# A DiT layer on one core: the second norm and the first seven-part product in another order on VectorE and ScalarE, two low parts on GpSimd

## The chip, the core and the metric

The kernel runs on one core of one Trainium2 chip. The metric is the time of one execution on the device, in microseconds (us). For the kernel before, it is 1764.85 us, the median of 3 runs that lie between 1764.47 and 1765.17 us.

## The reference

One layer of a diffusion backbone on 1024 latent tokens of width 1024, with 256 context tokens. Its first half (a recurrent branch, a windowed attention branch, their merge and the output projection) ends in the stream `x`. The change lies behind it, in the second half:

```python
x = x + g1 * merge_branches(y_rx, y_ax, gax, gbx, w_o_rnn[l], w_o_attn[l], w_out[l])
hx2 = modulate(rms_norm(x, norm2_w[l]), sh2, sc2)
x = x + g2 * conv_ffn(hx2, w_up[l], ffn_conv_w[l], ffn_conv_b[l], w_down[l])
...
def conv_ffn(h, w_up, conv_w, conv_b, w_down):
    u = dwconv(h @ w_up, conv_w, conv_b, FFN_CONV_W // 2)
    a, v = jnp.split(u, 2, axis=-1)
    return (jax.nn.gelu(a) * v) @ w_down
```

`h @ w_up` has 2 x 3072 output columns. The kernel holds channels on the partitions: a "row" is 128 channels x 1024 tokens, and rows come in 24 pairs of a gate row and a value row.

## The kernel before

**The split.** Every fp32 matrix product is made as three fp32r matmuls (lines 921 to 923): high x high, high x low, low x high. So every operand needs a high part (a rounding copy, mostly on ScalarE) and a low part (source minus high part, mostly on VectorE), and a tile can enter TensorE only when both are there.

**The second norm.** VectorE adds the projection to the stream (`add_out_half`, L2577), in halves of 512 tokens for the last two rows. The sums of squares go through TensorE (`square_columns`, L1333); VectorE adds them (`second_sum`, L2600), ScalarE takes the root (`second_root`), VectorE builds a diagonal from the reciprocal (`second_diagonal`, L2608), and TensorE spreads it over the partitions into PSUM (`spread`, L1343, two matmuls L1347 and L1348). This is done once for each half h of the tokens. Then for each of 8 row blocks k VectorE scales the stream (`normed`, L2590, tile yq), ScalarE makes the high part with the shift added (`normed_high`, tile B_hi), and VectorE the low part (`normed_low`, L2597, tile B_lo). For h = 0, `second_sum(1)` and `second_diagonal(1)` for the other half stand between these, ahead of k = 5 and k = 6.

**The plain products.** The first two pairs of rows are made as plain products (`plain_part`, L1364). Pair 0 follows the norm block by block, for h = 0 and then h = 1; `spread(1)` stands ahead of its k = 7. Pair 1 follows in one piece of 96 matmuls and needs its weights' high parts from ScalarE (`high_w`) and their low parts from VectorE (`plain_low`, L2653, tile wlo_both).

**The seven-part products.** The other 22 pairs are made by a seven-product scheme on 2 x 2 blocks (`fast_pair`, L1393). Each of the seven parts is 12 matmuls: 4 blocks x three matmuls. One operand is a block of the normed stream or one of the sums T1 to T4 (built once, tile T_sum, `t1f` to `t3f` and the lower left of yq), the other a weight block or a sum of two (`weight_sums`, tile wsum, lines 2700 to 2705), with high and low part (`fac_high`, `fac_low` L2711). The parts are taken in the order B11, T2, T3, T1, B21, T4, B22. The first product also needs T2, T3, T1 and T4 in high (`block_high`) and low parts (`block_low`, L2672), all four low parts on VectorE; T1, T2 and T3 have theirs written over the sums. ScalarE makes the high parts of the fifth and sixth weight block only behind the low part of T4.

**Around each pair**, ScalarE writes the centre tap of the convolution (tiles ca and cv), VectorE adds the two other taps (`taps_of` L2686 and L2689, `value_taps_of` L2715 and L2718), ScalarE applies GELU, VectorE multiplies (`product_of`, L2724), and the SP queue stores the row (`store_row`, L640). `up_step` (L2789 on VectorE, L2039 on ScalarE) writes out this order for the pairs from the second on. The centre of the next value row waits for the product before it, and the centre of the next gate row for the store to land.

Engines run their lists in written order and meet only at semaphores. `t_sum` counts the sums, `t_hi` and `t_lo` the high and low parts of the T blocks. In `fast_pair` the first product's waits are:

```python
if f in (1, 2, 3, 5):
    pe.wait_ge(S["t_lo"], AT["t_lo"] + {1: 1, 3: 2, 2: 3, 5: 4}[f])
```

GpSimd's last work in the kernel before is `add_half_square(1)` (L891), at about 1011 us.

Of the kernel before, what the change touches and what calls it, by code (L numbers as in the profile page):

```python
# [73 lines left out]
def build(nc, D, out):  # L74
# [199 lines left out]
    with ctx:  # L274
# [446 lines left out]
        def _(pool):  # L721
# [190 lines left out]
            add_half_square(1)  # L912


        @block.tensor
        def _(pe):
# [457 lines left out]
            for h in range(2):  # L1374
                for k in range(KC):
                    if h == 0 and k == 3:
                        square_columns(1)
                    elif h == 0 and k == KC - 1:
                        spread(1)
# [100 lines left out]
        def _(act):  # L1480
# [461 lines left out]
            normed_high(0, range(3, 5))  # L1942
            second_root(1)
            normed_high(0, range(5, KC))
# [3 lines left out]
            normed_high(1, range(KC))  # L1948
# [7 lines left out]
            block_high(T3, t3f[:, :, :], 4 * KQ)  # L1956
# [29 lines left out]
            gelu_of(0)  # L1986
            for f in (1, 2, 3):
                fac_high(1, 0, f)
            act.wait_ge(S["plain_full"], AT["plain_full"] + 3)
            act_of(ug[:, :], plain_row(1, 0), ACT.Copy).then_inc(S["row_copied"], 1)  # L1990
            act.wait_ge(S["plain_full"], AT["plain_full"] + 4)
            act_of(uv[:, :], plain_row(1, 1), ACT.Copy).then_inc(S["row_copied"], 1)
            block_high(T4, yq[:, KQ:, 0:HALF], 4 * KQ)
            for f in (4, 5):
                fac_high(1, 0, f)
# [120 lines left out]
        def _(dve):  # L2116
# [513 lines left out]
            for k in range(1, KC):  # L2630
                if k == 3:
                    add_out_half(KC - 1, 1)
                elif k == 5:
                    second_sum(1)
                elif k == 6:
                    second_diagonal(1)
# [13 lines left out]
            link(v.tensor_tensor(sh_diff[:, :], rest[:, 1, KQ:], rest[:, 1, 0:KQ], sub))  # L2650
            for k in range(KQ):
                v.tensor_tensor(t1f[:, k, :], yq[:, k, HALF:SEQ], yq[:, k, 0:HALF], sub).then_inc(S["t_sum"], 1)
# [5 lines left out]
            for c in range(2):  # L2658
                plain_low(c)
# [4 lines left out]
            for k in range(KQ):  # L2664
                dve.wait_ge(S["t_sum"], AT["t_sum"] + KQ + k + 1)
                v.scalar_tensor_tensor(out=yq[:, k + KQ, 0:HALF], in0=yq[:, k + KQ, 0:HALF],
                                       scalar=rest[:, 1, k + KQ:k + KQ + 1], in1=t2f[:, k, :], op0=add, op1=sub)\
                    .then_inc(S["t_sum"], 1)
# [4 lines left out]

            for k in range(KQ):
                v.scalar_tensor_tensor(out=t3f[:, k, :], in0=yq[:, k + KQ, HALF:SEQ], scalar=sh_diff[:, k:k + 1],
                                       in1=yq[:, k, HALF:SEQ], op0=add, op1=sub).then_inc(S["t_sum"], 1)
            dve.wait_ge(S["t_sum"], AT["t_sum"] + 3 * KQ)
            block_low(T2, t2f[:, :, :], 1)
            block_low(T1, t1f[:, :, :], 2)
# [273 lines left out]
```

## Time and profile before

| | us |
|---|---|
| median of 3 runs | 1764.85 |
| the profiled execution, on the device | 1765.58 |
| its span in the trace | 1763.8 |
| TensorE (matmul) busy | 1730.7 |
| VectorE busy | 1220.7 |
| ScalarE busy | 776.0 |
| GpSimd busy | 542.6 |

Times in the trace count from the start of the span. PE is TensorE, DVE is VectorE, ACT is ScalarE, POOL is GpSimd, SP is the queue that issues most transfers. The granted TensorE clock is full in all 40 slices of the span. Matmuls of 512 columns overlap, so a row's duration (0.39 us) is longer than the distance of two starts; places are therefore compared here by their start times. Where a row has a count above 1, its duration is that of the whole group.

### The profile page before, as it was taken

What the parts mean: (1) busy time and instruction counts of PE and PEld (TensorE: products, weight loads), DVE (VectorE), ACT (ScalarE), POOL (GpSimd) and SP (SyncE); (2) the same over time, 40 slices, a digit from 0 to 9 for tenths busy, and PEclk for the clock granted to TensorE, in tenths of its full rate; (3) what the DMA queues carried; (4) which work ended last, traced back from release to release, by engine and by line L of the source; (5) the groups of instructions that cost most, each with busy time, mean ns of one, the idle gap of its engine ahead of it and who ended that gap; (6) DMA issues with size and microseconds to landing.
All of it is one profiled execution on the core that took longest, in us unless ns stands there. A gap on an engine that the chain in (4) does not pass through costs nothing.

```text
span 1763.8 us, 23344 instructions
## 1 busy us (share of the span) xinstructions
PE 1730.7 (98%) x8382; PEld 1433.7 (81%) x8382; DVE 1220.7 (69%) x1386; ACT 776.0 (44%) x1017; POOL 542.6 (31%) x262
## 2 busy tenths in 40 slices
PE   7999999999999999989999999999999999999998
PEld 5897888887888888878888877888888888888887
DVE  7989767779316588867246389999999898424425
ACT  6358778788000288830011144444444444202205
POOL 1037766664336576625557700000000000000000
PEclk9999999999999999999999999999999999999999
DMA  9231111111453300057216312222222224523112
GB/s 370 78 114 45 51 52 51 61 52 43 167 193 96 84 13 0 1 197 248 80 59 251 124 54 96 84 95 83 88 78 83 78 82 161 203 105 128 54 37 96
DMA packets 56149, 177.98 MB, mean 101 GB/s; under 512 B 11794, under 2 KB 12178, under 8 KB 55444
## 3 DMA queue, kind: packets, MB, share of 16 engines
q1 hardware_dynamic: 46964, 148.27, 23.8%
q10 hardware_dynamic: 9120, 28.84, 5.0%
q8 instruction: 41, 0.67, 0.2%
q14 instruction: 24, 0.20, 0.0%
HBM read 140.39 MB, written 31.46 MB: 97 GB/s over the span
## 4 chain that ended last, share of the span: by engine, by line
PE 80%; DVE 7%; issue 2%; ACT 2%; DMA 1%; POOL 0%; SPq 0%; ACTq 0%; DVEq 0%; POOLq 0%
PE acc L921 17%; PE acc L922 17%; PE acc L923 17%; PE gp L921 8%; PE gp L922 8%; PE gp L923 8%; PE gp L1071 2%; PE acc L1249 1%; DMA wst<-in_w_in 1%; DVE r_lo L2353 1%; DVE y_lo L2371 1%; DVE T_lo L2672 0%; PE gp L1224 0%; PE gp L1223 0%; PE gp L1222 0%
## 5 line engine op out<-in xcount | busy, mean ns | idle before, releaser
L921 PE MATMUL acc<-hx_hi,whi_both 128*128 128x512 f32 x672 | 264.4, 393 | 3.5 <-ACT sg L1482 1.6
L922 PE MATMUL acc<-hx_lo,whi_both 128*128 128x512 f32 x672 | 261.8, 390 | 0.0
L923 PE MATMUL acc<-hx_hi,wlo_both 128*128 128x512 f32 x672 | 261.5, 389 | 0.0
L731 POOL TENSOR_TENSOR whi_both<-wst,ones 128x1024 fp32r<-128x1024 f32 x56 | 148.3, 2648 | 258.6 <-PE acc L923 244.8
L733 POOL TENSOR_TENSOR wlo_both<-wst,whi_both 128x1024 fp32r<-128x1024 f32 x56 | 174.2, 3111 | 4.4
L921 PEld LDWEIGHTS acc<-hx_hi,whi_both 128*128 128x128 f32 x672 | 126.1, 188 | 35.7 <-issue 4.6
L923 PEld LDWEIGHTS acc<-hx_hi,wlo_both 128*128 128x128 f32 x672 | 126.2, 188 | 26.6
L922 PEld LDWEIGHTS acc<-hx_lo,whi_both 128*128 128x128 f32 x672 | 126.2, 188 | 25.0
L1482 ACT ACTIVATE dn_hi<-wst 128x768 fp32r<-128x768 f32 x32 | 26.9, 844 | 182.8 <-PE acc L923 120.9
L921 PE MATMUL acc<-T_hi,fac_hi 128*128 128x512 f32 x264 | 102.8, 389 | 0.4 <-DVE fac_lo L2711 0.4
L923 PE MATMUL acc<-T_hi,fac_lo 128*128 128x512 f32 x264 | 102.7, 389 | 0.0
L922 PE MATMUL acc<-T_lo,fac_hi 128*128 128x512 f32 x264 | 102.7, 389 | 0.0
L2786 DVE SCALAR_TENSOR_TENSOR x1t<-acc,rest,x1t 128x1024 f32<-128x1024 f32 x16 | 20.5, 1281 | 101.8 <-PE acc L923 101.8
L921 PE MATMUL gp<-g_hi,dn_hi 128*128 128x512 f32 x192 | 74.9, 390 | 1.0 <-DVE dn_lo L2779 1.0
L922 PE MATMUL gp<-g_lo,dn_hi 128*128 128x512 f32 x192 | 74.7, 389 | 0.0
L923 PE MATMUL gp<-g_hi,dn_lo 128*128 128x512 f32 x192 | 74.7, 389 | 0.0
L921 PE MATMUL acc<-g_hi,dn_hi 128*128 128x512 f32 x192 | 74.7, 389 | 0.0
L922 PE MATMUL acc<-g_lo,dn_hi 128*128 128x512 f32 x192 | 74.7, 389 | 0.0
L923 PE MATMUL acc<-g_hi,dn_lo 128*128 128x512 f32 x192 | 74.7, 389 | 0.0
L1482 ACT ACTIVATE fac_hi<-wsum 128x512 fp32r<-128x512 f32 x88 | 51.8, 625 | 49.7 <-DVE wsum L2703 40.9
L921 PE MATMUL gp<-B_hi,fac_hi 128*128 128x512 f32 x176 | 68.5, 389 | 0.0
L922 PE MATMUL gp<-B_lo,fac_hi 128*128 128x512 f32 x176 | 68.5, 389 | 0.0
(403 smaller groups left out, 4624.6 us busy)
## 6 DMA issues: line engine op xcount, KB each, us to landing
wst<-in_w_in SPq DMA_DIRECT2D x43, 512.0 KB, 3.5
wst<-in_w_up SPq DMA_DIRECT2D x26, 512.0 KB, 4.2
wg<-in_mod_rest ACTq DMA_DIRECT2D x24, 512.0 KB, 5.3
ffn_row_scratch<-ca SPq DMA_DIRECT2D x24, 512.0 KB, 2.6
wst<-in_w_down SPq DMA_DIRECT2D x32, 384.0 KB, 3.1
g_in<-ffn_row_scratch SPq DMA_DIRECT2D x24, 512.0 KB, 7.0
wup<-in_w_up SPq DMA_DIRECT2D x22, 512.0 KB, 4.0
wmod<-in_mod_first SPq DMA_DIRECT2D x16, 512.0 KB, 15.5
```

Of the source, the lines that this page charges most:

```text
L731: nc.gpsimd.tensor_tensor(whi[s][:, 0:kc, :], wst[s][:, 0:kc, :], ones_of(kc), mult).then_inc(S["w_hi"], 1)
L733: nc.gpsimd.tensor_tensor(wlo[s][:, 0:kc, :], wst[s][:, 0:kc, :], whi[s][:, 0:kc, :], sub)\
L921: mm(out_ap, w_h, x_h, start=first, stop=False)
L922: mm(out_ap, w_h, x_l, start=False, stop=False)
L923: return mm(out_ap, w_l, x_h, start=False, stop=last)
L1071: last = mm(bank[:, o:o + wide], w[rows, d, :], x[rows, x0:x0 + wide], start=t == 0, stop=t == 2)
L1249: last = nc.tensor.transpose(pt_bank(j)[:, P * h:P * (h + 1)], prob[kh][:, h, P * kb:P * (kb + 1)], ident[:, :])
L1482: return nc.scalar.activation(o, x, f, **kw)
L2353: v.tensor_tensor(r_lo[c][:, :], Y[:, c, :], r_hi[c][:, :], sub).then_inc(S["y_lo_s"], 1)
L2371: v.tensor_tensor(dst[:, c, :], src[:, c, :], hi[:, c, :], sub).then_inc(S[lo_sem], 1)
L2786: v.scalar_tensor_tensor(out=x1t[m][:, :], in0=o_bank(n), scalar=rest[:, 3, m:m + 1], in1=x1t[m][:, :], op0=mult, op1=add).then_inc(S["dn_ ...
```

## The change

It changes no arithmetic result of any tile, only the order of instructions and, for two of them, the engine.

- Second norm, first half: `second_sum(1)` and `second_diagonal(1)` stand one block later on VectorE (ahead of k = 6 and k = 7); `spread(1)` one block earlier on TensorE (ahead of k = 6); on ScalarE the root stands behind one more high part.
- ScalarE makes the high parts of the second half's blocks 0 to 2 ahead of the first weight copy, and block 3 between the two copies.
- VectorE makes the first plain low part ahead of the sums T1, and the sums T3 ahead of the sums T4.
- The low parts of T1 and T3 are made by GpSimd, behind the low part of T2, which stays on VectorE.
- VectorE makes the weight sums and the first weight blocks' low parts, with T2's, ahead of the taps of pair 0; the product of pair 0 stands behind the low parts of T4 and of weight blocks 4 and 5.
- ScalarE copies the first row of pair 1 ahead of weight blocks 1 to 3, and the GELU of pair 0 stands behind T4's high part.

```diff
--- before.py
+++ after.py
@@ -910,6 +910,10 @@
             for c in range(2):
                 split_plain(c)
             add_half_square(1)
+            pool.wait_ge(S["t_lo"], AT["t_lo"] + 1)
+            for blk, total, count in ((T1, t1f, 2), (T3, t3f, 3)):
+                pool.wait_ge(S["t_hi"], AT["t_hi"] + count)
+                nc.gpsimd.tensor_tensor(blk[1][:, :, :], total[:, :, :], blk[0][:, :, :], sub).then_inc(S["t_lo"], 1)
 
 
         @block.tensor
@@ -1375,7 +1379,7 @@
                 for k in range(KC):
                     if h == 0 and k == 3:
                         square_columns(1)
-                    elif h == 0 and k == KC - 1:
+                    elif h == 0 and k == KC - 2:
                         spread(1)
                     for c in range(2):
                         last = plain_part(0, c, h, (k,), plain_hi[c], plain_lo[c])
@@ -1939,13 +1943,15 @@
             half_square(KC - 2, 1)
             normed_high(0, range(3))
             half_square(KC - 1, 1)
-            normed_high(0, range(3, 5))
+            normed_high(0, range(3, 6))
             second_root(1)
-            normed_high(0, range(5, KC))
+            normed_high(0, range(6, KC))
+            normed_high(1, range(3))
             full(act, A_S5 + KC - 1)
             for c in range(2):
                 high_w(W_S6 + 2 + c, "w_ready", W_S6 + 2)
-            normed_high(1, range(KC))
+                normed_high(1, (3 + c,))
+            normed_high(1, range(5, KC))
 
             def block_high(blk, src, sums):
                 act.wait_ge(S["t_sum"], AT["t_sum"] + sums)
@@ -1953,7 +1959,7 @@
 
             block_high(T2, t2f[:, :, :], 2 * KQ)
             block_high(T1, t1f[:, :, :], KQ)
-            block_high(T3, t3f[:, :, :], 4 * KQ)
+            block_high(T3, t3f[:, :, :], 3 * KQ)
 
             def centre_of(p, src):
                 act_of(ca[:, :], src, ACT.Identity, scale=conv_col(1, 0, p), bias=ffn_col(C_FCB, p)).then_inc(S["f_centre"], 1)
@@ -1983,14 +1989,14 @@
             act.wait_ge(S["plain_full"], AT["plain_full"] + 2)
             value_centre_of(0, plain_row(0, 1))
             fac_high(1, 0, 0)
-            gelu_of(0)
+            act.wait_ge(S["plain_full"], AT["plain_full"] + 3)
+            act_of(ug[:, :], plain_row(1, 0), ACT.Copy).then_inc(S["row_copied"], 1)
             for f in (1, 2, 3):
                 fac_high(1, 0, f)
-            act.wait_ge(S["plain_full"], AT["plain_full"] + 3)
-            act_of(ug[:, :], plain_row(1, 0), ACT.Copy).then_inc(S["row_copied"], 1)
             act.wait_ge(S["plain_full"], AT["plain_full"] + 4)
             act_of(uv[:, :], plain_row(1, 1), ACT.Copy).then_inc(S["row_copied"], 1)
             block_high(T4, yq[:, KQ:, 0:HALF], 4 * KQ)
+            gelu_of(0)
             for f in (4, 5):
                 fac_high(1, 0, f)
             act.wait_ge(S["row_copied"], AT["row_copied"] + 2)
@@ -2630,9 +2636,9 @@
             for k in range(1, KC):
                 if k == 3:
                     add_out_half(KC - 1, 1)
-                elif k == 5:
+                elif k == 6:
                     second_sum(1)
-                elif k == 6:
+                elif k == 7:
                     second_diagonal(1)
                 normed(0, k)
                 normed_low(0, k - 1)
@@ -2647,38 +2653,27 @@
 
             dve.wait_ge(S["n2_a"], 2 * KC)
             dve.sem_inc(acc_read[A_ST2 % 2], 1)
-            link(v.tensor_tensor(sh_diff[:, :], rest[:, 1, KQ:], rest[:, 1, 0:KQ], sub))
-            for k in range(KQ):
-                v.tensor_tensor(t1f[:, k, :], yq[:, k, HALF:SEQ], yq[:, k, 0:HALF], sub).then_inc(S["t_sum"], 1)
             def plain_low(c):
                 n0 = W_S6 + 2 + c
                 dve.wait_ge(S["w_hi"], n0 + 1)
                 v.tensor_tensor(wlo[n0 % 2][:, :, :], wst[n0 % 2][:, :, :], whi[n0 % 2][:, :, :], sub).then_inc(S["w_ready"], 1)
 
-            for c in range(2):
-                plain_low(c)
+            plain_low(0)
+            link(v.tensor_tensor(sh_diff[:, :], rest[:, 1, KQ:], rest[:, 1, 0:KQ], sub))
+            for k in range(KQ):
+                v.tensor_tensor(t1f[:, k, :], yq[:, k, HALF:SEQ], yq[:, k, 0:HALF], sub).then_inc(S["t_sum"], 1)
+            plain_low(1)
             for k in range(KQ):
                 dve.wait_ge(S["t_sum"], AT["t_sum"] + k + 1)
                 v.scalar_tensor_tensor(out=t2f[:, k, :], in0=yq[:, k + KQ, HALF:SEQ], scalar=rest[:, 1, k + KQ:k + KQ + 1],
                                        in1=t1f[:, k, :], op0=add, op1=sub).then_inc(S["t_sum"], 1)
             for k in range(KQ):
-                dve.wait_ge(S["t_sum"], AT["t_sum"] + KQ + k + 1)
-                v.scalar_tensor_tensor(out=yq[:, k + KQ, 0:HALF], in0=yq[:, k + KQ, 0:HALF],
-                                       scalar=rest[:, 1, k + KQ:k + KQ + 1], in1=t2f[:, k, :], op0=add, op1=sub)\
-                    .then_inc(S["t_sum"], 1)
+                v.scalar_tensor_tensor(out=t3f[:, k, :], in0=yq[:, k + KQ, HALF:SEQ], scalar=sh_diff[:, k:k + 1],
+                                       in1=yq[:, k, HALF:SEQ], op0=add, op1=sub).then_inc(S["t_sum"], 1)
 
             def block_low(blk, src, count):
                 dve.wait_ge(S["t_hi"], AT["t_hi"] + count)
                 v.tensor_tensor(blk[1][:, :, :], src, blk[0][:, :, :], sub).then_inc(S["t_lo"], 1)
-
-            for k in range(KQ):
-                v.scalar_tensor_tensor(out=t3f[:, k, :], in0=yq[:, k + KQ, HALF:SEQ], scalar=sh_diff[:, k:k + 1],
-                                       in1=yq[:, k, HALF:SEQ], op0=add, op1=sub).then_inc(S["t_sum"], 1)
-            dve.wait_ge(S["t_sum"], AT["t_sum"] + 3 * KQ)
-            block_low(T2, t2f[:, :, :], 1)
-            block_low(T1, t1f[:, :, :], 2)
-            dve.wait_ge(S["t_sum"], AT["t_sum"] + 4 * KQ)
-            block_low(T3, t3f[:, :, :], 3)
 
             def taps_of(p, src):
 
@@ -2723,15 +2718,25 @@
                 dve.wait_ge(S["v_conv"], AT["v_conv"] + p + 1)
                 v.tensor_tensor(ca[:, :], ca[:, :], cv[:, :], mult).then_inc(S["f_prod"], 1)
 
+            for k in range(KQ):
+                dve.wait_ge(S["t_sum"], AT["t_sum"] + KQ + k + 1)
+                v.scalar_tensor_tensor(out=yq[:, k + KQ, 0:HALF], in0=yq[:, k + KQ, 0:HALF],
+                                       scalar=rest[:, 1, k + KQ:k + KQ + 1], in1=t2f[:, k, :], op0=add, op1=sub)\
+                    .then_inc(S["t_sum"], 1)
+            weight_sums(1, 0)
+            fac_low(1, 0, 0)
+            dve.wait_ge(S["t_sum"], AT["t_sum"] + 4 * KQ)
+            block_low(T2, t2f[:, :, :], 1)
+            fac_low(1, 0, 1)
+            for f in (2, 3):
+                fac_low(1, 0, f)
             taps_of(0, plain_row(0, 0))
-            weight_sums(1, 0)
-            for f in range(4):
-                fac_low(1, 0, f)
             value_taps_of(0, plain_row(0, 1))
-            product_of(0)
+            dve.wait_ge(S["t_lo"], AT["t_lo"] + 3)
             block_low(T4, yq[:, KQ:, 0:HALF], 4)
             for f in (4, 5):
                 fac_low(1, 0, f)
+            product_of(0)
 
             def top_right(e, i):
```

VectorE, second norm of the first half, before: `COPY` and the next row are `second_sum(1)`, the rows from `RECIPROCAL` to `diag_lo` are `second_diagonal(1)`; yq rows are `normed`, B_lo rows `normed_low`.

```order
516 L2603 COPY rstd_61<-gp 128x4
517 L2606 TENSOR_TENSOR rms<-gp,rstd_61 128x4
518 L2590 SCALAR_TENSOR_TENSOR yq<-yq,a2col,acc 128x512
519 L2597 SCALAR_TENSOR_TENSOR B_lo<-yq,rest,B_hi 128x512
520 L2612 RECIPROCAL rstd_61<-rms 128x4
```

The same place in the changed kernel:

```order
516 L2596 SCALAR_TENSOR_TENSOR yq<-yq,a2col,acc 128x512
517 L2603 SCALAR_TENSOR_TENSOR B_lo<-yq,rest,B_hi 128x512
518 L2609 COPY rstd_61<-gp 128x4
519 L2612 TENSOR_TENSOR rms<-gp,rstd_61 128x4
520 L2596 SCALAR_TENSOR_TENSOR yq<-yq,a2col,acc 128x512
521 L2603 SCALAR_TENSOR_TENSOR B_lo<-yq,rest,B_hi 128x512
522 L2618 RECIPROCAL rstd_61<-rms 128x4
```

One `normed` and one `normed_low` now stand ahead of the sum that they followed.

VectorE, from the end of the norm to the first weight block's low part, before (T_sum and yq x4 are the sums T1, T2, T4, T3):

```order
543 L2650 TENSOR_TENSOR sh_diff<-rest 128x4
544 L2652 TENSOR_TENSOR T_sum<-yq 128x512 x4
545 L2656 TENSOR_TENSOR wlo_both<-wst_74,whi_both 128x1024
546 L2656 TENSOR_TENSOR wlo_both<-wst_73,whi_both 128x1024
547 L2662 SCALAR_TENSOR_TENSOR T_sum<-yq,rest,T_sum 128x512 x4
548 L2666 SCALAR_TENSOR_TENSOR yq<-yq,rest,T_sum 128x512 x4
549 L2675 SCALAR_TENSOR_TENSOR T_sum<-yq,sh_diff 128x512 x4
550 L2672 TENSOR_TENSOR T_lo<-T_sum,T_hi 128x2048 x3
551 L2686 SCALAR_TENSOR_TENSOR ca<-gp,pcol,ca 128x1023
552 L2689 SCALAR_TENSOR_TENSOR ca<-gp,pcol,ca 128x1023
553 L2700 TENSOR_TENSOR wsum_255<-wst_74 128x512
```

The changed kernel:

```order
554 L2706 TENSOR_TENSOR fac_lo_248<-wst_73,fac_hi_241 128x512
555 L2676 TENSOR_TENSOR T_lo<-T_sum,T_hi 128x2048
556 L2706 TENSOR_TENSOR fac_lo_249<-wsum_256,fac_hi_242 128x512
557 L2706 TENSOR_TENSOR fac_lo_250<-wsum_257,fac_hi_243 128x512
558 L2706 TENSOR_TENSOR fac_lo_251<-wsum_255,fac_hi_244 128x512
559 L2681 SCALAR_TENSOR_TENSOR ca<-gp,pcol,ca 128x1023
560 L2684 SCALAR_TENSOR_TENSOR ca<-gp,pcol,ca 128x1023
561 L2710 SCALAR_TENSOR_TENSOR cv<-gp,pcol,cv 128x1023
562 L2713 SCALAR_TENSOR_TENSOR cv<-gp,pcol,cv 128x1023
563 L2676 TENSOR_TENSOR T_lo<-yq,T_hi 128x2048
564 L2706 TENSOR_TENSOR fac_lo_252<-wst_73,fac_hi_245 128x512
565 L2706 TENSOR_TENSOR fac_lo_253<-wst_74,fac_hi_246 128x512
```

Ahead of these stand, in the changed kernel, one plain low part, `sh_diff`, the four sums T1, the other plain low part, the sums T2, T3 and T4 and the four weight sums. Of the three low parts of T1 to T3 one is left on VectorE. The other two are the last rows of GpSimd:

```order
227 L896 TENSOR_TENSOR ssum<-ssum,sqb 128x512
228 L916 TENSOR_TENSOR T_lo<-T_sum,T_hi 128x2048 x2
229 L274 UNCONDITIONAL_BRANCH
```

Nothing moved ahead of them: GpSimd has been out of work since the half square.

## Rows read from the trace of the kernel before

**Rows 1.** The page: busy time of each engine, then the chain that ended last, by engine.

```profile
PE 1730.7 (98%) x8382; PEld 1433.7 (81%) x8382; DVE 1220.7 (69%) x1386; ACT 776.0 (44%) x1017; POOL 542.6 (31%) x262
...
PE 80%; DVE 7%; issue 2%; ACT 2%; DMA 1%; POOL 0%; SPq 0%; ACTq 0%; DVEq 0%; POOLq 0%
```

**Rows 2.** Who waited for whom: TensorE from 975 to 1100 us (total, times, longest).

```profile
PE gp L921 <- DVE B_lo L2597: 2.5, 2, 1.5
PE acc L921 <- DVE wlo_both L2656: 1.4, 1, 1.4
```

**Rows 3.** The timeline: TensorE (start, duration; in brackets idle before it and its releaser).

```profile
1024.94 0.50 PE L921 MATMUL gp<-B_hi,plain_hi 128*128 128x512 f32 x1 [1.48 <-DVE B_lo L2597]
...
1030.83 0.50 PE L921 MATMUL gp<-B_hi,plain_hi 128*128 128x512 f32 x1 [1.02 <-DVE B_lo L2597]
...
1043.47 0.47 PE L921 MATMUL acc<-B_hi,whi_both 128*128 128x512 f32 x1 [1.45 <-DVE wlo_both L2656]
...
1065.11 0.39 PE L923 MATMUL acc<-B_hi,wlo_both 128*128 128x512 f32 x1
1066.09 0.47 PE L921 MATMUL acc<-B_hi,fac_hi 128*128 128x512 f32 x1 [0.60 <-ACT ug L1482]
...
1088.54 0.50 PE L921 MATMUL acc<-T_hi,fac_hi 128*128 128x512 f32 x1 [0.41 <-DVE fac_lo L2711]
```

**Rows 4.** The timeline: VectorE, from the second norm to the second product.

```profile
1019.38 0.16 DVE L2603 COPY rstd<-gp 128x4 f32<-128x4 f32 x1 [1.48 <-PE gp L1331]
...
1025.46 1.63 DVE L2597 SCALAR_TENSOR_TENSOR B_lo<-yq,rest,B_hi 128x512 fp32r<-128x512 f32 x2
1028.49 1.41 DVE L2590 SCALAR_TENSOR_TENSOR yq<-yq,a2col,acc 128x512 f32<-128x512 f32 x2 [1.39 <-PE acc L1348]
...
1039.69 2.50 DVE L2652 TENSOR_TENSOR T_sum<-yq 128x512 f32<-128x512 f32 x4
1042.11 2.35 DVE L2656 TENSOR_TENSOR wlo_both<-wst,whi_both 128x1024 fp32r<-128x1024 f32 x2
...
1052.33 6.68 DVE L2672 TENSOR_TENSOR T_lo<-T_sum,T_hi 128x2048 fp32r<-128x2048 f32 x3
...
1061.44 0.68 DVE L2700 TENSOR_TENSOR wsum<-wst 128x512 f32<-128x512 f32 x1
...
1063.97 0.69 DVE L2711 TENSOR_TENSOR fac_lo<-wst,fac_hi 128x512 fp32r<-128x512 f32 x1
1064.58 1.89 DVE L2711 TENSOR_TENSOR fac_lo<-wsum,fac_hi 128x512 fp32r<-128x512 f32 x3
...
1069.08 1.22 DVE L2724 TENSOR_TENSOR ca<-ca,cv 128x1024 f32<-128x1024 f32 x1
1070.22 2.28 DVE L2672 TENSOR_TENSOR T_lo<-yq,T_hi 128x2048 fp32r<-128x2048 f32 x1
...
1075.44 0.69 DVE L2711 TENSOR_TENSOR fac_lo<-wsum,fac_hi 128x512 fp32r<-128x512 f32 x1 [0.89 <-ACT fac_hi L1482]
...
1087.81 1.89 DVE L2711 TENSOR_TENSOR fac_lo<-wsum,fac_hi 128x512 fp32r<-128x512 f32 x3
```

**Rows 5.** Groups by line and shape: GpSimd (count, busy us, mean ns).

```profile
L825 POOL TENSOR_TENSOR q_lo<-yq,q_hi 128x512 fp32r<-128x512 f32 x16 | 20.8, 1298 | 2.3 <-POOL q_hi L823 1.8
...
L904 POOL TENSOR_TENSOR plain_lo<-wst,plain_hi 128x1024 fp32r<-128x1024 f32 x2 | 4.8, 2392 | 0.2
```

**Rows 6.** The timeline: VectorE from 957.5 to 962 us.

```profile
957.56 3.22 DVE L2513 SCALAR_TENSOR_TENSOR wgr<-wgr,crow 128x1024 f32<-128x1024 f32 x1
...
960.71 1.27 DVE L2574 SCALAR_TENSOR_TENSOR yq<-acc,rest,xres 128x1024 f32<-128x1024 f32 x1
```

**Rows 7.** The timeline: GpSimd in the same stretch.

```profile
959.78 3.27 POOL L733 TENSOR_TENSOR wlo_both<-wst,whi_both 128x1024 fp32r<-128x1024 f32 x1
```

**Rows 8.** The timeline: ScalarE, centre of the second value row.

```profile
1073.66 1.23 ACT L1482 ACTIVATE cv<-uv,pcol 128x1024 f32<-128x1024 f32 x1
```

**Rows 9.** DMA issues from 1498.9 to 1499.2 us (count, KB each, us to landing).

```profile
ffn_row_scratch<-ca SPq DMA_DIRECT2D x1, 512.0 KB, 3.1
```

## The prediction

> **What bounds the kernel now.** I read the page first. TensorE is busy 98% of the span and holds 80% of the chain that ended last [rows 1]. The change gives TensorE no matmul more or less, so it can win only time in which TensorE stands still between its units of work. The second view is who waited for whom on TensorE around the change: 2.5 us for low parts of the norm and 1.4 us for a plain low part [rows 2]. The third, TensorE's own timeline, says where: it restarts late at 1024.94, 1030.83 and 1043.47, at 1066.09 (the first seven-part product) and at 1088.54 (second part of the second one). The idle times there are 1.48, 1.02, 1.45, 0.60 and 0.41 us, together 5.0 us, 0.28% of the span [rows 3]. Four of the five name VectorE. So the last view is VectorE's timeline. The reader is to see that it runs from 1028.49 to 1088.5 with two pauses only, one of them 0.89 us at 1075.44 [rows 4]. The last stop, at 1088.54, is where that list and TensorE meet for the last time: whatever TensorE gains before, it gives back there unless VectorE arrives earlier too. I therefore compute that meeting twice, and the change of the time is its shift; behind it both kernels run the same lists, and the waits of TensorE up to the down projection end with it.
>
> **Norm, second half.** VectorE stands idle for 1.48 us ahead of the row at 1019.38, since it needs the columns from TensorE, which are not moved. One `normed` and one `normed_low` now fall into that pause: 2 x 0.66 us of starts (half of a pair that takes 1.41 and 1.63 us with overlap). Its first half then ends at 1025.46 + 1.63 - 1.3 = 1025.8. The spread stood ahead of k = 7 and is now ahead of k = 6; its diagonal is ready where it was, three starts of 0.66 us ahead of the row at 1025.46, at about 1023.6; TensorE is then in k = 5, so the spread is done by 1024.8, and VectorE goes on at 1025.8 with no wait, where it began at 1028.49 [rows 4]: 2.7 us earlier. TensorE followed that start by 1030.83 - 1028.49 = 2.34 us, so it starts the half at 1028.1. Of the wait at 1024.94 I expect some 0.3 us left, in front of k = 6.
>
> **Plain rows of pair 1.** The two weight copies on ScalarE now stand between high parts; that pushes VectorE by at most a copy's overlap, which I take as 0.2 us. TensorE needs 48 x 0.227 = 10.9 us for the half; the 0.227 comes from 1043.47 to 1065.11, 95 starts of a 96-matmul product, less the slow first [rows 3]. It is through at 1039.0. The plain low part comes first on VectorE now, at 1025.8 + (1039.69 - 0.19 - 1028.49) + 0.2 = 1037.0, and is there at 1038.2: the wait of 1.45 us is gone. The 96 matmuls start at 1039.0 where they started at 1043.47, and end at 1060.8. The wait of 0.60 us for the copied row goes as well, since ScalarE copies it at 1053 and TensorE comes at 1060.8, 5.3 us earlier than 1066.09.
>
> **VectorE up to T2's low part.** From 1028.49 to the three low parts at 1052.33 it needed 23.84 us; the same list now runs from 1025.8 to 1049.8. Weight sums 1063.97 - 1061.44 = 2.5 us, half a us for ScalarE, whose high parts come first, the first weight block 0.6, T2's low part 2.2 (a third of 6.68 us) [rows 4]: 1055.6.
>
> **The low parts on GpSimd.** No row shows a 128x2048 subtraction there. 128x512 takes 1298 ns and 128x1024 2392 ns [rows 5], so 1.09 us for each 512 more, 4.6 us for 2048 and 9.2 us for two, against 2.2 us each that VectorE saves. The rows also show that the two engines slow each other: a VectorE operation with two inputs in SBUF took 3.22 us beside GpSimd [rows 6], where two plain low parts of the same size took 2.35 us together [rows 4], and GpSimd took 3.27 instead of 2.39 us [rows 7]. An operation with one input in PSUM took 1.27 us beside the same GpSimd row [rows 6]: not slowed. GpSimd starts at 1055.7. Three weight low parts of 512 fall beside it: VectorE needs 1.6 instead of 0.6 us for each, 4.9 us together, and GpSimd loses 3 x 0.44 = 1.3 us. The four taps of pair 0 read PSUM, so they cost their old 2.5 + 2.6 us. VectorE is ready for T4 at 1065.7; GpSimd ends at 1055.7 + 9.2 + 1.3 = 1066.2, and VectorE waits half a us for it. The bounds of the term: 9.2 us without mutual slowing, 12.5 us with it all through (3.27 / 2.39). I take 10.5, since only the three low parts have the shape of the slowed row. TensorE wants T3 at 1060.8 + 24 x 0.227 = 1066.2, just then, so at most a short wait, which the meeting hides.
>
> The Trainium skill (GPSIMD Engine Reference, 3.1) speaks against the move: it measures a 2048-element fp32 addition at 4497 ns on GpSimd and 2293 ns on VectorE and keeps elementwise work on VectorE. By its figure, an estimate, the term would be 9.0 + 1.3 us and the sum 0.2 us better than mine. Its specification table (section 1) also says that GpSimd shares SBUF interfaces with VectorE and collides with operations that have two SBUF inputs; by that rule the taps escape, and the trace agrees with 1.27 us.
>
> **To the meeting.** T4's low part 2.3 us, then ScalarE's high part of block 4 (0.7 with the hand-over), which only starts behind it: 1069.2. Blocks 4 and 5 1.2 us, product 1.2 us: 1071.6. Then a hand-over that was hidden: the next value centre on ScalarE waits for the product. Before, it began at 1073.66 [rows 8], 3.4 us behind the product at 1069.08 + 1.22, because of T4 and the weight blocks; from its start to the seventh weight block's low part on VectorE is 1075.44 - 1073.66 = 1.8 us [rows 4]. So this low part starts at 1073.4. From it to the low part that TensorE awaits, VectorE's list is full and unchanged: 1088.54 - 1075.44 = 13.1 us. Meeting at 1086.5 to 1086.9, say 1086.7.
>
> **The sum.** TensorE could be there at 1060.8 + 96 x 0.227 = 1082.6, and will stand still about 4.1 us. The meeting moves from 1088.54 to 1086.7: **1.8 us earlier**. In VectorE's terms, which give 1.9 with their rounding: -2.7 for the norm, -4.4 for two low parts given away and -0.9 for the old pause at 1075.44; against these +3.1 for the slowed weight blocks, +0.5 for the wait for GpSimd, +0.2 and +0.5 for ScalarE in the norm and ahead of the first weight block, and +1.8 for the centre behind the product. The profiled execution took 1765.58 us, 0.7 above the median; against it I expect 1763.8, against the median **1763.0**. That is 0.10%. Less than 0.2%, 3.5 us, cannot be told from no change here, so this counts as no change.
>
> **Rivals.**
> (a) GpSimd and VectorE don't slow each other over these tiles. VectorE is at T4 at 1062.5 and waits for GpSimd until 1064.9: meeting 1.3 us earlier still, 1761.7. For it: nothing but the different tiles. Against: 3.22 and 3.27 us. Chance 0.15.
> (b) Slower: GpSimd's work becomes the bound. If the taps are slowed like the low parts, all of GpSimd's stretch is contended and ends at 1055.7 + 12.5 = 1068.2; VectorE has by then done 12.5 / 2.6 = 4.8 of its 6.9 us and is at T4 at 1070.3, 4.1 us behind my sum: 1767.1. It decides from a VectorE arrival at T4 later than 1068.0, which cancels the 1.8 us. Against it: 1.27 us [rows 6]. Chance 0.12.
> (c) The store of pair 0's row. The next gate centre waits for it to land, and the loads for pair 3, which used to be issued 4 us behind it, now follow at once. A store with loads right behind landed after 3.1 us [rows 9]. Issued at 1071.7 it lands at 1074.8; with 1.2 us for the centre it is 0.6 us ahead of the taps that need it at about 1076.6. Each us more costs one: at 4.3 us the time is 1763.6. Chance 0.15.
> (d) The half does not start earlier, because something other than the spread holds it (the change does not do what it says): VectorE's 2.7 us are lost and the meeting is 0.9 us later than before, 1765.8. Against: the pause at 1019.38 is real and long enough. Chance 0.06.
> (e) TensorE sets the meeting after all, at 1082.7: 1759.0. VectorE would have to save 4 us that no row offers. Chance 0.04.
>
> **How the numbers follow.** My forecast has 0.48. The predicted time is its time. For 8 in 10 the range runs from (a) with 0.5 us of repeat scatter, 1761.2, to (d) with 0.4, 1766.2; (b) and (e) lie outside. Faster by over 0.2% (below 1761.3) is (e) and the tail of (a): 0.09. Slower by over 0.2% (above 1768.4) needs (b) with slower subtractions than 3.27 us per 1024: 0.06. The rest, 0.85, is no change.
>
> **What would show it.** In the changed profile: VectorE's second half starting near 1025.8; TensorE restarting at 1039 with no wait for a plain low part and starting the seven-part product near 1060.8; two GpSimd rows of 4.6 to 6 us from 1055.7; three VectorE low parts of about 1.6 us beside them and taps still at 1.28; one pause of TensorE of some 4 us near 1082.6 on `fac_lo`. The sum is wrong if that pause is absent or if TensorE waits on T3 longer than 1 us; the reasons are wrong if the time moves and these starts do not.

## The result and the profile after

| | before | after |
|---|---|---|
| median, 8 runs each, us | 1765.01 | **1770.94** |
| lowest to highest | 1764.47 to 1768.03 | 1769.79 to 1771.96 |
| profiled execution, device | 1765.58 | 1769.79 |
| its span | 1763.8 | 1768.0 |

The ratio is 1.0029 with a 95% interval of 1.0020 to 1.0039: the change costs about 5.9 us. I had forecast 1763.0, within 1761.2 and 1766.2, and called it no change. The forecast is wrong, in size and in sign.

The first page lines of the changed kernel and the shares of its chain [rows 1]:

```profile
PE 1733.4 (98%) x8382; PEld 1436.0 (81%) x8382; DVE 1223.1 (69%) x1384; ACT 778.4 (44%) x1017; POOL 556.9 (31%) x264
...
PE 80%; DVE 6%; ACT 3%; issue 2%; DMA 1%; POOL 0%; SPq 0%; ACTq 0%; DVEq 0%; POOLq 0%
```

GpSimd's busy time is up by 14.3 us, of which 10 are the two low parts (the rest lies ahead of the change). VectorE's is up by 2.4 us, though it gave away two operations of 2.2 us. TensorE's is up by 2.7 us, with the same 8382 matmuls. Both engines have done the same or less work in more time; that is the first clue.

Who TensorE waited for, from 975 to 1480 us [rows 2]:

```profile
PE acc L925 <- DVE fac_lo L2706: 3.7, 1, 3.7
PE gp L925 <- DVE fac_lo L2706: 3.1, 1, 3.1
PE acc L1351 <- DVE diag_lo L2623: 0.8, 1, 0.8
```

The waits for `B_lo` and `wlo_both` are gone, as the change wants. Two waits for a weight block's low part have taken their place, each longer than any that was there before.

VectorE's timeline in the changed kernel [rows 4] (the three weight low parts one by one):

```profile
1018.74 0.16 DVE L2609 COPY rstd<-gp 128x4 f32<-128x4 f32 x1 [0.15 <-PE gp L1335]
...
1025.05 1.40 DVE L2596 SCALAR_TENSOR_TENSOR yq<-yq,a2col,acc 128x512 f32<-128x512 f32 x2
...
1052.64 2.29 DVE L2676 TENSOR_TENSOR T_lo<-T_sum,T_hi 128x2048 fp32r<-128x2048 f32 x1
1054.85 0.68 DVE L2706 TENSOR_TENSOR fac_lo<-wsum,fac_hi 128x512 fp32r<-128x512 f32 x1
1055.45 5.09 DVE L2706 TENSOR_TENSOR fac_lo<-wsum,fac_hi 128x512 fp32r<-128x512 f32 x1
1060.47 5.10 DVE L2706 TENSOR_TENSOR fac_lo<-wsum,fac_hi 128x512 fp32r<-128x512 f32 x1
1065.49 1.27 DVE L2681 SCALAR_TENSOR_TENSOR ca<-gp,pcol,ca 128x1023 f32<-128x1023 f32 x1
...
1070.51 2.28 DVE L2676 TENSOR_TENSOR T_lo<-yq,T_hi 128x2048 fp32r<-128x2048 f32 x1
...
1077.87 0.69 DVE L2706 TENSOR_TENSOR fac_lo<-wsum,fac_hi 128x512 fp32r<-128x512 f32 x1 [1.89 <-ACT fac_hi L1486]
```

GpSimd's timeline beside it:

```profile
1055.01 4.99 POOL L916 TENSOR_TENSOR T_lo<-T_sum,T_hi 128x2048 fp32r<-128x2048 f32 x1 [43.34 <-DVE T_lo L2676]
...
1059.96 5.07 POOL L916 TENSOR_TENSOR T_lo<-T_sum,T_hi 128x2048 fp32r<-128x2048 f32 x1
```

Read the two together. The first weight low part was running when GpSimd began, and took 0.68 us. The second was issued at 1055.45, inside GpSimd's first instruction, and ended at 1060.54: 0.54 us, its own length, after that instruction's end at 1060.00. The third ended at 1065.57, 0.54 us after the end of the second one at 1065.03. Three operations of 0.6 us took 10.7 us.

TensorE's timeline at the two pauses [rows 3]:

```profile
1074.29 0.50 PE L925 MATMUL gp<-B_hi,fac_hi 128*128 128x512 f32 x1 [3.05 <-DVE fac_lo L2706]
...
1090.97 0.50 PE L925 MATMUL acc<-T_hi,fac_hi 128*128 128x512 f32 x1 [3.71 <-DVE fac_lo L2706]
1091.31 0.39 PE L926 MATMUL acc<-T_lo,fac_hi 128*128 128x512 f32 x1
...
1092.62 0.63 PE L925 MATMUL acc<-T_hi,fac_hi 128*128 128x512 f32 x1
1093.04 0.63 PE L926 MATMUL acc<-T_lo,fac_hi 128*128 128x512 f32 x1
```

The second pause ends at the meeting of the prediction: 1088.54 before, 1086.7 forecast, 1090.97 here. From about 1.3 us behind the restart matmuls start 0.43 us apart for a while, where they had started 0.23 us apart. A view in stretches shows why (busy us of the engines with counts, then granted clock, DMA share, GB/s):

```profile
1093.00:1095.00 2.00, 2.00 (x6) 1.57 (x5) 2.00 (x4) 1.04 (x1) 0.00 (x0) 0.50 0.00 0
...
1097.00:1110.00 13.00, 13.00 (x59) 10.75 (x58) 12.86 (x17) 4.64 (x8) 0.00 (x0) 1.00 0.23 91
```

For some 3 us TensorE is granted half its clock, 1.2 instead of 2.4 GHz. From the meeting to the next place where TensorE waits for VectorE (the down projection) the changed kernel needs 1495.03 - 1090.97 = 404.06 us and the one before 1490.99 - 1088.54 = 402.45, for the same list. So the lower clock costs 1.6 us in this execution. The row at 1495.03 ends this stretch:

```profile
1495.03 0.50 PE L925 MATMUL gp<-g_hi,dn_hi 128*128 128x512 f32 x1 [0.95 <-DVE dn_lo L2784]
```

and the same in the kernel before:

```profile
1490.99 0.50 PE L921 MATMUL gp<-g_hi,dn_hi 128*128 128x512 f32 x1 [0.95 <-DVE dn_lo L2779]
```

### The profile page after: what moved, and what is told of

It is laid out like the page before. It is cut to its first block, busy times and chain, and to the rows that moved or that the text cites. A ratio compares the mean times of both kernels' runs of the same rounds, so it can differ in the third digit from the quotient of the medians.

```text
span 1768.0 us, 23345 instructions
## 1 busy us (share of the span) xinstructions
PE 1733.4 (98%) x8382; PEld 1436.0 (81%) x8382; DVE 1223.1 (69%) x1384; ACT 778.4 (44%) x1017; POOL 556.9 (31%) x264
## 4 chain that ended last, share of the span: by engine, by line
PE 80%; DVE 6%; ACT 3%; issue 2%; DMA 1%; POOL 0%; SPq 0%; ACTq 0%; DVEq 0%; POOLq 0%
PE acc L925 17%; PE acc L927 17%; PE acc L926 17%; PE gp L925 8%; PE gp L927 8%; PE gp L926 8%; PE gp L1075 2%; PE acc L1253 1%; DVE fac_lo L2706 1%; DMA wst<-in_w_in 1%; DVE y_lo L2377 1%; ACT sr L1486 1%; PE gp L1228 0%; PE gp L1227 0%; PE gp L1226 0%
## 5 line engine op out<-in xcount | busy, mean ns | idle before, releaser
L731 POOL TENSOR_TENSOR whi_both<-wst,ones 128x1024 fp32r<-128x1024 f32 x56 | 152.1, 2715 | 258.0 <-PE acc L927 244.6
L925 PE MATMUL gp<-B_hi,fac_hi 128*128 128x512 f32 x176 | 69.2, 393 | 3.1 <-DVE fac_lo L2706 3.1
L2300 DVE SCALAR_TENSOR_TENSOR qq<-qq,sr 128x1280 f32<-128x1280 f32 x16 | 43.4, 2720 | 40.1 <-ACT sr L1486 40.1
```

What stands on the lines that cost most here:

```text
L731: nc.gpsimd.tensor_tensor(whi[s][:, 0:kc, :], wst[s][:, 0:kc, :], ones_of(kc), mult).then_inc(S["w_hi"], 1)
L925: mm(out_ap, w_h, x_h, start=first, stop=False)
L2300: v.scalar_tensor_tensor(out=qq[d][:, :], in0=qq[d][:, :], scalar=1.0, in1=sr[d][:, :], op0=add, op1=mult)\
```

## The experiments

The theory after the result: (A) a VectorE operation with two inputs in SBUF is not slowed beside GpSimd, it stands until GpSimd's running instruction has ended. The rival: (B) VectorE runs at a share of its speed, and 128x2048 tiles are merely worse than 128x1024. Beside these stood the question which parts of the new order pay, and what the pauses cost. During the experiments the kernel before ran at 1765.26 to 1765.39 us. Where places of two kernels are compared, they are taken from the `COPY` row of `second_sum(1)` (1018.74 above), since the part ahead of it ends between 1018.5 and 1020.7 us in the profiles here. Part of that spread is the clock too: in the three profiles in which this row stands later than 1019.5 us, the granted clock was 0.91 from 740 to 760 or from 780 to 800 us, far ahead of the change (as it was in a fourth, with the row at 1019.11).

**GpSimd's instructions in quarters.** One edit, each low part in four instructions of 128x512:

```diff
-                nc.gpsimd.tensor_tensor(blk[1][:, :, :], total[:, :, :], blk[0][:, :, :], sub).then_inc(S["t_lo"], 1)
+                for k in range(KQ):
+                    ins = nc.gpsimd.tensor_tensor(blk[1][:, k, :], total[:, k, :], blk[0][:, k, :], sub)
+                ins.then_inc(S["t_lo"], 1)
```

> The changed kernel with each of GpSimd's two low parts in four instructions of 128x512 instead of one of 128x2048. Theory A (a VectorE operation with two SBUF inputs stands still until the GpSimd instruction that runs has ended): the three weight low parts beside it take about 1.8 us each instead of 5, the seven-part product's fifth part no longer waits, and the time falls by 4 to 5 us against the changed kernel, to 1766 or 1767. Rival B (both engines run on at a fixed share of their speed, whatever the length of an instruction): no change, 1771, and the three low parts stay at 10.7 us together.

Measured: 1766.40 us, ratio 1.0005 (0.9995 to 1.0014). VectorE's timeline:

```profile
1056.03 0.68 DVE L2708 TENSOR_TENSOR fac_lo<-wsum,fac_hi 128x512 fp32r<-128x512 f32 x1
...
1056.63 1.78 DVE L2708 TENSOR_TENSOR fac_lo<-wsum,fac_hi 128x512 fp32r<-128x512 f32 x1
...
1058.33 1.78 DVE L2708 TENSOR_TENSOR fac_lo<-wsum,fac_hi 128x512 fp32r<-128x512 f32 x1
...
1067.56 2.29 DVE L2678 TENSOR_TENSOR T_lo<-yq,T_hi 128x2048 fp32r<-128x2048 f32 x1 [2.43 <-POOL T_lo L917]
```

and GpSimd's:

```profile
1056.19 1.67 POOL L917 TENSOR_TENSOR T_lo<-T_sum,T_hi 128x512 fp32r<-128x512 f32 x1 [43.33 <-DVE T_lo L2678]
...
1057.82 1.74 POOL L917 TENSOR_TENSOR T_lo<-T_sum,T_hi 128x512 fp32r<-128x512 f32 x1
```

The same low part on VectorE takes 0.68 us ahead of GpSimd's work, 1.78 beside instructions of 1.7 us and 5.09 beside one of 4.99. A share of speed would not depend on the length of the other's instruction. So (A) holds: the end is again that of GpSimd's instruction plus 0.55 us (1056.19 + 1.67 + 0.55 = 1058.41 = 1056.63 + 1.78). The same bytes in shorter pieces bring back 4.5 us of the time, although GpSimd becomes slower by it (eight pieces take 11.3 us) and VectorE then waits 2.43 us for it. In this profile, of an execution 1.6 us above the median, the granted clock was 0.50 for longer than in the changed kernel's, and the stretch from the meeting (1088.04) to the down projection took 405.0 us:

```profile
1087.00:1093.00 6.00, 4.96 (x12) 3.90 (x13) 5.37 (x10) 1.97 (x3) 0.00 (x0) 0.50 0.19 64
```

**The weight blocks ahead of T2.** No operation with two SBUF inputs is left beside GpSimd, only the taps:

```diff
-            block_low(T2, t2f[:, :, :], 1)
-            fac_low(1, 0, 1)
-            for f in (2, 3):
+            for f in (1, 2, 3):
                 fac_low(1, 0, f)
+            block_low(T2, t2f[:, :, :], 1)
```

> The changed kernel with the low parts of weight blocks 1 to 3 ahead of T2's low part, so that beside GpSimd VectorE has only the taps, which read PSUM. Theory A: taps at 1.28 us although GpSimd runs, GpSimd's two rows at 4.6 us, and T3 is there at about 1066; time 1766 to 1767. Rival B, with taps slowed too: taps at 2 us or more and 1768 or more.

Measured: 1767.00 us, ratio 1.0009 (1.0000 to 1.0019). VectorE's timeline:

```profile
1059.22 1.28 DVE L2684 SCALAR_TENSOR_TENSOR ca<-gp,pcol,ca 128x1023 f32<-128x1023 f32 x1
1060.42 1.27 DVE L2710 SCALAR_TENSOR_TENSOR cv<-gp,pcol,cv 128x1023 f32<-128x1023 f32 x1
1061.72 1.28 DVE L2713 SCALAR_TENSOR_TENSOR cv<-gp,pcol,cv 128x1023 f32<-128x1023 f32 x1
...
1067.29 2.29 DVE L2676 TENSOR_TENSOR T_lo<-yq,T_hi 128x2048 fp32r<-128x2048 f32 x1 [4.28 <-POOL T_lo L916]
```

GpSimd by line and shape (count, busy us, mean ns):

```profile
L916 POOL TENSOR_TENSOR T_lo<-T_sum,T_hi 128x2048 fp32r<-128x2048 f32 x2 | 9.2, 4618 | 46.0 <-DVE T_lo L2676 46.0
```

The taps, with one input in PSUM, keep their 1.28 us, and GpSimd its undisturbed 4618 ns, which is the 4.6 us that the prediction had drawn from the smaller shapes [rows 5]. Yet the gain is only 4 us of the 5.9: VectorE now stands 4.28 us for GpSimd, and TensorE 1.2 us for T3's low part. The low parts are simply twice as long there, and T4 has to wait for all of them.

**The order alone.** Everything on VectorE again, T1 and T3 behind the third weight block; the rest of the new order stays:

```diff
-            pool.wait_ge(S["t_lo"], AT["t_lo"] + 1)
...
             for f in (2, 3):
                 fac_low(1, 0, f)
+            block_low(T1, t1f[:, :, :], 2)
+            block_low(T3, t3f[:, :, :], 3)
             taps_of(0, plain_row(0, 0))
             value_taps_of(0, plain_row(0, 1))
-            dve.wait_ge(S["t_lo"], AT["t_lo"] + 3)
```

> The changed kernel with the low parts of T1 and T3 back on VectorE, behind weight block 3; all else of the new order stays. If GpSimd's part is what costs (theory A): three weight low parts of 0.6 us, product of pair 0 at about 1070, TensorE's pause ahead of the second product's second part ends near 1086, time 1765 to 1766 against 1765.0 before and 1770.9 changed. Rival C (the new order alone loses the time, through the centre behind the product and the long pause): 1769 or more.

Measured: 1765.92 us, ratio 1.0003 (0.9994 to 1.0012). The two low parts on GpSimd cost 5.0 us, by the medians of the changed kernel and this one. But the order alone gains nothing either. VectorE's timeline has the five low parts in 6.4 us, back to back, and further on a wait:

```profile
1055.10 1.89 DVE L2702 TENSOR_TENSOR fac_lo<-wsum,fac_hi 128x512 fp32r<-128x512 f32 x3
1056.90 4.49 DVE L2672 TENSOR_TENSOR T_lo<-T_sum,T_hi 128x2048 fp32r<-128x2048 f32 x2
...
1073.69 0.69 DVE L2702 TENSOR_TENSOR fac_lo<-wsum,fac_hi 128x512 fp32r<-128x512 f32 x1 [1.89 <-ACT fac_hi L1482]
```

TensorE's waits have:

```profile
PE acc L921 <- DVE fac_lo L2702: 4.1, 2, 3.7
```

These two say where the 2.7 us for the norm went. VectorE waits 1.89 us, where it waited 0.89 [rows 4], because the value centre on ScalarE has moved behind the product. And TensorE, which is early, spends its lead in one pause of 3.7 us. A third wait lies ahead of the first weight block's low part, the half us that the sum had forecast for ScalarE there:

```profile
1052.29 0.69 DVE L2702 TENSOR_TENSOR fac_lo<-wst,fac_hi 128x512 fp32r<-128x512 f32 x1 [0.46 <-ACT fac_hi L1482]
```

**The norm alone.** The kernel before, with the edits of the second norm and of ScalarE's list around the weight copies, and nothing else (on TensorE and VectorE):

```diff
-                    elif h == 0 and k == KC - 1:
+                    elif h == 0 and k == KC - 2:
                         spread(1)
...
-                elif k == 5:
-                    second_sum(1)
                 elif k == 6:
+                    second_sum(1)
+                elif k == 7:
                     second_diagonal(1)
```

> The kernel before with only the edits on the second norm (sum and diagonal one block later, spread one block earlier, high parts ahead of the weight copies). By my sum: VectorE's second half starts 2.7 us earlier and everything up to the second product follows, 1762.5 (1762 to 1763), faster than both kernels. Rival D (the norm's gain is hidden or lost elsewhere): 1765.

Measured: **1762.23 us, ratio 0.9983 (0.9974 to 0.9992)**, faster by 3.1 us. TensorE's waits from 975 to 1480 us:

```profile
PE acc L921 <- DVE wlo_both L2658: 1.5, 1, 1.5
PE acc L1347 <- DVE diag_lo L2619: 0.8, 1, 0.8
PE acc L921 <- ACT ug L1482: 0.6, 1, 0.6
PE acc L921 <- DVE fac_lo L2713: 0.4, 1, 0.4
```

The meeting, from the `COPY` row on, comes after 66.4 us instead of 69.2: 2.7 us earlier, exactly the term of the sum. The waits stay spread and short.

**The norm, and one high part earlier.** On top of it, ScalarE makes the high part of the seventh weight block ahead of the value centre, so that VectorE doesn't wait for it:

```diff
             for f in (4, 5):
                 fac_high(1, 0, f)
+            fac_high(1, 0, 6)
```

(`up_step` leaves it out for that pair.)

> The kernel before with the edits on the second norm, and on ScalarE the high part of the seventh weight block of the first seven-part product ahead of the value centre of pair 1. VectorE's pause of 0.9 us ahead of that block's low part goes; the meeting with TensorE is 0.6 us earlier, 1761.6 against 1762.2. If something else ends that stretch: 1762.2.

Measured: 1761.66 us, ratio 0.9983 (0.9974 to 0.9992), the lowest of all kernels here. The wait for `fac_lo` is gone from TensorE's list, the other three rows read as above. The meeting is 65.8 us behind the `COPY` row, 0.6 earlier; the two intervals overlap fully, so by the times this step alone isn't shown.

**The product back in its place.** The order alone, with `product_of(0)` ahead of T4's low part:

```diff
             value_taps_of(0, plain_row(0, 1))
+            product_of(0)
             block_low(T4, yq[:, KQ:, 0:HALF], 4)
             for f in (4, 5):
                 fac_low(1, 0, f)
-            product_of(0)
```

> The kernel with the new order but all low parts on VectorE, and the product of pair 0 ahead of T4's low part again. If the wait of 1.9 us of VectorE for the value centre behind the product is a real cost: that wait shrinks to below 1 us, the second product's second part starts about 0.8 us earlier, 1765.1. If it is hidden: 1765.9.

Measured: 1765.31 us, ratio 1.0000 (0.9991 to 1.0009). VectorE's wait falls back to 0.88 us and the meeting comes 0.8 us earlier from the `COPY` row (67.0 against 67.8). The times move by 0.6 us in the same direction, within the intervals, so by the times this isn't shown.

**The pause of the order alone, filled.** 17 pairs of small matmuls on `ones` stand in the pause of TensorE; their results are overwritten. If the clock falls because of the pause, this keeps it up:

```diff
                 for f, blk in enumerate((B11, T2, T3, T1, B21, T4, B22)):
+                    if begin and f == 4:
...
+                        keep_running(up_bank[4], 0)
+                    elif isinstance(w, int) and w == 2 and f == 1:
+                        pe.wait_ge(S["u2_done"], AT["u2_done"] + 1)
+                        keep_running(up_bank[1], 17)
```

> The kernel with the new order but all low parts on VectorE, with 17 small matmuls in its one long pause. Theory E: the full clock, 1764, against 1765.9 without them, so the new order alone is about 1 us better than the kernel before as long as the clock holds. Rival F: 1765.9.

Measured: 1764.39 us, ratio 0.9996 (0.9987 to 1.0005), against 1765.92 without the fill. The stretch behind the pause, without it in the first fence and with it in the second (the granted clock is the third number from the end):

```profile
1086.50:1091.00 4.50, 4.21 (x11) 3.31 (x12) 4.44 (x8) 1.22 (x2) 0.00 (x0) 0.62 0.00 0
```

```profile
1086.50:1091.00 4.50, 4.50 (x21) 3.65 (x21) 3.90 (x7) 1.76 (x3) 0.00 (x0) 1.00 0.10 15
```

From the meeting to the down projection this kernel needs 402.5 us, the unfilled one 404.1. That is the 1.5 us by which the medians differ; the intervals of the two overlap, so the rows carry this reading more than the times do. That the new order is better than the kernel before once the clock holds, as expected, isn't shown: the interval contains 1.

**Both pauses of the changed kernel, filled, twice.** First with 13 pairs ahead of the fifth part of the first product (the line with the 0 above) and 24 at the second:

> The changed kernel with small matmuls (ones x ones, 13 and 24 of 128 columns) in TensorE's two long pauses, into the bank that the next part writes over. Theory E (behind a pause TensorE runs for some us at the lower clock, and that is the part of the loss beyond the shifted meeting of 3.1 us): granted clock at its full level throughout, 1768 against 1770.9. Rival F (the clock is not the cause, or the pauses cost what they cost): 1770 to 1771.

Measured: 1770.58 us, ratio 1.0032 (1.0020 to 1.0044). A miss, and one that says little: the second fill was too long. TensorE's timeline:

```profile
1086.94 5.52 PE L960 MATMUL acc<-ones 128*128 128x128 f32 x48
...
1092.22 0.48 PE L925 MATMUL acc<-T_hi,fac_hi 128*128 128x512 f32 x1
```

The product went on when the fill ended, at 1092.22, over a us late. So again with 13 and 17:

> The same with 13 and 17 small matmuls: the 24 of the first try ran 1.4 us past the moment at which VectorE was ready (TensorE went on at 1092.22 instead of about 1090.8). Theory E (the lower clock behind a pause costs 1.6 us and more): second product's second part starts at 1090.9, full clock behind it, 1768.5 to 1769.2. Rival F: 1770.6 to 1771.

Measured: 1769.24 us, ratio 1.0021 (1.0012 to 1.0030). The stretches behind both pauses are at full clock:

```profile
1075.00:1079.00 4.00, 4.00 (x19) 3.31 (x18) 2.11 (x4) 1.76 (x2) 0.00 (x0) 1.00 0.47 147
1091.00:1100.00 9.00, 9.00 (x42) 7.43 (x42) 8.33 (x12) 3.90 (x5) 0.00 (x0) 1.00 0.33 119
```

The changed kernel beside it, once more as it is:

> The changed kernel once more, on the same chip as the filled one: 1770.9, with a mean granted clock of 0.995 to 0.997.

Measured: 1771.31 us, ratio 1.0030 (1.0019 to 1.0042): the result repeats, and the fill takes off 2.1 us, or 1.7 against the first median. The intervals of the two ratios overlap. What speaks for the clock in all executions, and not only in the profiled ones, is its mean: 0.998 to 0.999 in the 11 with the fill, 0.995 to 0.998 in the 15 without. In its profile the same two stretches read:

```profile
1075.00:1079.00 4.00, 2.77 (x8) 2.18 (x9) 2.43 (x3) 1.97 (x3) 0.00 (x0) 0.78 0.07 26
1091.00:1100.00 9.00, 7.10 (x24) 5.71 (x25) 8.30 (x13) 4.17 (x6) 0.00 (x0) 0.81 0.43 153
```

## Why the prediction was wrong

**Right, to about a tenth: the part up to 1055.** The changed kernel's front part runs 0.64 us early (`COPY` at 1018.74 against 1019.38); with that added, VectorE's second half starts at 1025.7 (forecast 1025.8), the seven-part product at 1060.8 with no wait (1060.8), T2's low part ends at 1055.6 (1055.6). Behind it the taps take 1.28 us, as forecast. The kernel with the norm alone shows the -2.7 us by itself. GpSimd's pair takes 10.0 us against 10.5: near in size, though not by the mechanism of the sum.

**The step that failed** is in "The low parts on GpSimd": "VectorE needs 1.6 instead of 0.6 us for each, 4.9 us together". They took 10.7, so the term of +3.1 us measures 10.7 - 1.8 = 8.9. I read the row of 3.22 us [rows 6] as a rate, 2.6 times slower. It was a wait. GpSimd's timeline of the kernel before has, ahead of the row I quoted [rows 7], this one:

```profile
956.82 2.88 POOL L731 TENSOR_TENSOR whi_both<-wst,ones 128x1024 fp32r<-128x1024 f32 x1 [1.79 <-PE acc L923]
```

It ends at 959.70. The VectorE row began at 957.56 and ended at 960.78: 2.14 us of standing and 1.08 of work. One more row of the trace, read for its end and not only for its name, would have given the mechanism. The sum by it: two of the three weight low parts stand in turn behind GpSimd's two instructions, so VectorE is done with them at 1055.7 + 9.2 + 0.6 = 1065.5; with 5.1 us of taps it comes to T4 at 1070.6, 4.4 us behind my 1066.2. That is later than 1068.0, the point from which rival (b) said that the gain is gone. Measured, with the 0.64 added: 1071.15, 4.9 us behind.

The Trainium skill (SBUF — State Buffer, "SBUF: two separate sides" and "Who interferes with whom") states this: the port pair that the two engines share is an exclusive lock, whoever starts first has it for its whole instruction, and a VectorE operation with two SBUF inputs blocks fully against a GpSimd operation that reads SBUF. The trace agrees (5.09, 5.10 and 1.78 us, and the first low part, which started first, 0.68).

**Rival (b)** put the danger in the right place and priced it wrongly: it wanted the taps slowed, and they were not; the three small low parts were enough. Its 1767.1 is 3.8 us too low, and I had given it 0.12.

**The wait for GpSimd ahead of T4** (+0.5 us in the sum) did not appear, since VectorE came late itself. **Rival (c)** did not decide: ScalarE waited 1.15 us for the store, and VectorE's taps ran on without a stop. **Rivals (a), (d) and (e)** are out.

**The second missing term is the clock.** I forecast one pause "of some 4 us" and priced it at nothing, because the change of the time was to be the shift of the meeting and "behind it both kernels run the same lists". They do, but not at the same clock: 1.6 us in the profile.

The account, from the `COPY` row on, in the profiled executions:

| step | meeting behind `COPY`, us | shift |
|---|---|---|
| before | 69.2 | |
| norm alone | 66.4 | -2.7 |
| the whole order, on VectorE | 67.8 | +1.3 |
| the changed kernel | 72.2 | +4.5 |

With +1.6 for the clock behind the meeting and -0.6 for the earlier front part, this makes 4.0 us of the span's 4.2 (the meeting is 3.07 later). The +4.5 is the waiting for GpSimd: VectorE's three weight and two T low parts took 1.89 + 4.49 us in the order alone, and the three weight low parts by themselves took 10.7 in the changed kernel.

These are the profiled executions, and the changed kernel's is its fastest of 8; the medians lie 5.9 us apart, 1.2 more than meeting and clock together. The second profile of the changed kernel repeats both terms (72.2 and 404.05 us) in an execution of 1771.97 us. What that execution has on top, 2.2 us, lies almost all ahead of the change: its `COPY` row is 2.0 us later, with the lower clock from 740 to 760 us named above. Whether the 1.2 us of the medians come from there isn't shown.

Of the +1.3, 0.8 goes with the product's place; the other 0.5 is as large as VectorE's wait of 0.46 us for ScalarE's first high part, which neither the kernel before nor the one with the norm alone has. No run removed that wait by itself.

What stays open: the refilled kernel is 3.9 us above the one before, its meeting only 3.1; in its profile the part from ScalarE's last output rows to the end is 0.9 us longer (7.7 against 6.8), and the final stores took 4.2 us to land instead of 3.2. Whether that holds for its other runs isn't known. Combining the norm's edits with a pair of GpSimd low parts placed where VectorE has no two-input work was not tried.

## What to carry to other kernels

When two engines meet in a trace and one row is too long, lay its start and end against the other engine's instructions one by one, before reading a ratio out of it; a rate and a wait give the same row and very different sums. Work given to an idle engine must be priced by what it stops: here small operations that stood ahead of everything else waited for long ones that nobody needed yet. And where an edit moves waiting time from several short waits into one long pause, ask what TensorE's clock does behind it. Here one part of the change, the norm alone, is better than the whole.

## What the runs showed of the hardware

- A VectorE subtraction with two SBUF inputs, 0.6 us alone, took 5.09 and 5.10 us beside GpSimd instructions of 4.99 and 5.07 us, 1.78 beside those of about 1.7. It ends 0.54 to 0.55 us behind the other's end. GpSimd loses about VectorE's turn by it: 4.99 and 5.07 instead of 4.62 us.
- The two engines alternated by instruction here: GpSimd's second low part could not keep VectorE's waiting one out, though it was ready.
- Operations with one input in PSUM took 1.27 to 1.28 us beside GpSimd.
- Around pauses of 3.0 to 3.7 us TensorE's granted clock fell to 0.50, for some 3 us. In the two profiles of the changed kernel it fell 0.9 to 1.4 us behind the restart, in the order alone 0.7 us behind it. With the product back it fell 0.4 us ahead of the restart, and with GpSimd's quarters 1.4 us ahead of it, there for almost 7 us. The dip behind the later pause cost 1.4 to 1.6 us (403.9 to 404.1 instead of 402.45 us up to the down projection) and the long one 2.6. The dip behind the earlier pause was hidden, since TensorE waited for VectorE again.
- Behind the pauses of up to 1.5 us around the change in the kernel before the clock stayed at 1.00. It did not fall each time behind a long one: in the profile of the kernel with the weight blocks first it stayed at 1.00 behind 3.73 us. Small matmuls in the pause kept it up.
